# RWKV-7 recurrence of a backbone block: key and value products moved to the idle quarters of the TensorE array

## The reference, cut to what matters

```python
def rwkv7_scan(S0, r, decay, k, v, kk, a, reverse):
    def step(S, inp):
        r_t, w_t, k_t, v_t, kk_t, a_t = inp
        sa = jnp.einsum('bhvk,bhk->bhv', S, -kk_t)
        S = (S * w_t[:, :, None, :] + sa[..., None] * (kk_t * a_t)[:, :, None, :]
             + v_t[..., None] * k_t[:, :, None, :])
        return S, jnp.einsum('bhvk,bhk->bhv', S, r_t)
```

## Time and profile before

| | us |
|---|---|
| median of 3 runs | 2715.4 |
| lowest, highest | 2714.63, 2723.09 |
| the profiled execution | 2723.21 |
| its span | 2721.5 |
| mean granted TensorE clock | 0.928 of full speed |

### The profile page before, as it was taken

How to read it: one execution, slowest core, us unless ns; L and a number is a source line. 1 busy time by engine, 2 the same in 40 slices (tenths; PEclk the granted TensorE clock), 3 DMA queues, 4 the chain that set the end, 5 groups by cost and what they waited for, 6 DMA issues and landing times. The chain is left out here.

```text
span 2721.5 us, 60797 instructions
## 1 busy us (share of the span) xinstructions
PE 2415.9 (89%) x26659; PEld 1980.0 (73%) x26659; DVE 1147.7 (42%) x1601; ACT 804.3 (30%) x1329; POOL 458.1 (17%) x335
## 2 busy tenths in 40 slices
PE   5899985899999999996979999999797777899999
PEld 3668763788888888895868888888574445588887
DVE  4532323555555655643242222222348663433333
ACT  2232322343342343222153211221332332442231
POOL 0221213543543443520000000000111000000000
PEclk8889895799999999997989999999898998999999
DMA  9565650000000000003112221222110002233332
GB/s 309 169 207 176 191 175 24 21 23 9 28 23 8 29 22 9 9 10 124 53 47 62 68 70 56 62 67 64 47 32 23 0 0 62 62 96 105 89 105 84
DMA packets 261694, 191.86 MB, mean 70 GB/s; under 512 B 11610, under 2 KB 251876, under 8 KB 260964
## 3 DMA queue, kind: packets, MB, share of 16 engines
q1 hardware_dynamic: 261476, 188.58, 22.8%
HBM read 170.73 MB, written 17.83 MB: 69 GB/s over the span
## 5 line engine op out<-in xcount | busy, mean ns | idle before, releaser
L493 PE MATMUL bank<-operand_hi,ffn_hi 128*128 128x512 f32 (+1 forms) x1056 | 378.4, 358 | 25.7 <-DVE operand_lo L455 25.7
L486 DVE TENSOR_TENSOR ffn_lo<-ffn_raw,ffn_hi 128x1024 fp32r<-128x1024 f32 (+1 forms) x120 | 159.8, 1332 | 572.0 <-ACT ffn_hi L481 571.9
L494 PE MATMUL bank<-operand_lo,ffn_hi 128*128 128x512 f32 (+1 forms) x1056 | 377.5, 358 | 0.0
L495 PE MATMUL bank<-operand_hi,ffn_lo 128*128 128x512 f32 (+1 forms) x1056 | 374.9, 355 | 0.0
L481 ACT CAST ffn_hi<-ffn_raw 128x1024 fp32r<-128x1024 f32 (+1 forms) x120 | 136.4, 1136 | 531.4 <-PE bank L495 531.2
L1499 POOL TENSOR_TENSOR lvl<-sc,level_mask 128x512 f32<-128x512 f32 x144 | 203.9, 1423 | 441.9 <-PE bank L1124 407.8
L493 PEld LDWEIGHTS bank<-operand_hi,ffn_hi 128*128 128x128 f32 x1056 | 200.3, 190 | 62.7 <-issue 22.4
L495 PEld LDWEIGHTS bank<-operand_hi,ffn_lo 128*128 128x128 f32 x1056 | 199.7, 189 | 29.9
L494 PEld LDWEIGHTS bank<-operand_lo,ffn_hi 128*128 128x128 f32 x1056 | 200.4, 190 | 27.2
L494 PE MATMUL bank<-ffn_g_lo,ffn_hi 128*128 128x512 f32 (+1 forms) x528 | 188.0, 356 | 0.0
L493 PE MATMUL bank<-ffn_g_hi,ffn_hi 128*128 128x512 f32 (+1 forms) x528 | 187.4, 355 | 0.0
(11 more groups left out here) (243 smaller groups left out, 4660.8 us busy)
## 6 DMA issues: line engine op xcount, KB each, us to landing
mod_raw<-in_mod_w SPq DMA_DIRECT2D x96, 512.0 KB, 6.2
ffn_raw<-in_ff_w SPq DMA_DIRECT2D x88, 512.0 KB, 3.9
ffn_raw<-in_ff_w SPq DMA_DIRECT2D x32, 704.0 KB, 4.5
proj_raw<-in_rw_wr SPq DMA_DIRECT2D x8, 512.0 KB, 4.5
proj_raw<-in_rw_wk SPq DMA_DIRECT2D x8, 512.0 KB, 4.6
proj_raw<-in_rw_wv SPq DMA_DIRECT2D x8, 512.0 KB, 5.0
rwkv_out_raw<-in_rw_wo SPq DMA_DIRECT2D x8, 512.0 KB, 3.8
qk_w_raw<-in_at_wq SPq DMA_DIRECT2D x8, 512.0 KB, 3.7
```

The lines of the kernel that those rows point to most:

```text
L486: signal(eng, eng.tensor_tensor(self.lo[s][:, 0:k_tiles, :], self.raw[s][:, 0:k_tiles, :], self.hi[s][:, 0:k_tiles, :].bitcast(F32), ALU.s ...
L493: pe.matmul(out, w[0], x[0], start=first, stop=False)
L494: pe.matmul(out, w[0], x[1], start=False, stop=False)
L495: return pe.matmul(out, w[1], x[0], start=False, stop=last)
```

## The change

The key half of each score, the turned keys and the turned values are written to the other head's partitions, so head 0 uses the upper right quarter of the array and head 1 the lower left one. b and k are issued alternately, into a bank each (`B_BANK`, `K_BANK`), and `sc` splits into `sc_b` and `sc_k`. Scores are made for two steps at a time, two times a group instead of four; VectorE masks each bank on its own, so there are still four masks of 512 columns a group. Keys are turned with b in one call (`turn_keys`).

The three products of a step that need keys and values alone (key scores times values, keys times values, values times key scores for the output) leave `rhs` and `sy`. They are made one step ahead (`early_part`), in the off-diagonal quarters, two matmuls after each of the first six pairs of the inverse's `y`. `CHAIN` becomes two banks that alternate by step, and `rhs` and `sy` add to what `early_part` began. The last slot has no inverse and issues them alone. New waits: `y` waits for the outputs' state products of the present step (`y_opened`), and `rhs` and the output part of `sy` for the early products (`early_done`).

The banks for this come from `SIDE`, `T_BANK` and `X_BANK`: they become two `WORK` banks, through which `t`, `y` and all side pieces rotate, each waiting for the reader of the use before last.

```diff
-        Y_BANK, CHAIN, SIDE, SC_BANK = c.bank[0:2], c.bank[2], c.bank[3], c.bank[4:6]
-        T_BANK, X_BANK = c.bank[6], c.bank[7]
+        Y_BANK, CHAIN, B_BANK, K_BANK, WORK = c.bank[0:2], c.bank[2:4], c.bank[4], c.bank[5], c.bank[6:8]
...
+                def following(q):
+                    return (C, q + 1) if C and q < GROUP - 1 else (B, 0) if B and q == GROUP - 1 else None
...
                 if C:
                     E.u(C, 0)
-                if B:
-                    y(B, 2)
-                if A:
-                    score(A, 1)
+                y(B, 2, following(0))
                 extra(1)
                 if C:
                     E.sy(C, 0)
                 if A:
-                    score(A, 2)
+                    score(A, 1)
                 extra(2)
                 if C:
                     E.rhs(C, 1)
                 if B:
                     t(B, 3), cut(B, 5)
                 if A:
-                    score(A, 3), cut(A, 0), cut(A, 1)
+                    cut(A, 0), cut(A, 1)
                 extra(3)
                 if C:
                     E.u(C, 1)
-                if B:
-                    y(B, 3)
+                y(B, 3, following(1))
                 if A:
-                    turn(A, 0)
+                    turn_keys(A)
...
                 if B:
                     t(B, 4)
                 if A:
-                    level0(A), cut(A, 2), turn(A, 1)
+                    level0(A), cut(A, 2)
                 extra(6)
                 if C:
                     E.u(C, 2)
-                if B:
-                    y(B, 4)
+                y(B, 4, following(2))
                 if A:
-                    turn(A, 2)
+                    turn_values(A)
...
+                    def work_free(self, *key):
+                        n = self.use.of("work", *key)
                         if n >= 2:
-                            kind, g, i = self.use.key["bank", n - 2]
...
+                    def score(self, G, i):
...
+                        for q in (2 * i, 2 * i + 1):
+                            for e in range(2):
+                                n = G.chunk(q, e)
+                                tokens, at = slice(n * CH, n * CH + CH), 128 * (2 * (q % 2) + e)
                                 for h in range(2):
+                                    pe.matmul(B_BANK[half(h), at:at + 2 * CH], b_in[G.pair][e][half(h), tokens],
+                                              ar[G.pair][e][half(h), n, :, :], start=True, stop=True)
+                                for h in range(2):
+                                    mm = pe.matmul(K_BANK[half(1 - h), at:at + 2 * CH], k_in[G.pair][e][half(h), tokens],
                                                    ar[G.pair][e][half(h), n, :, :], start=True, stop=True)
                         mm.then_inc(scores, 1)
...
+                    def y(self, G, n, step):
+                        bank = self.work_free("y", G.g, n)
                         pe.wait_ge(t_copied, self.use.of("t", G.g, n) + 1)
+                        if step:
+                            self.early_waits(*step)
                         for w in range(2 * GROUP):
                             for h in range(2):
-                                mm = pe.matmul(X_BANK[half(h), w * CH:w * CH + CH], t_sb[G.parity][half(h), w, :],
+                                mm = pe.matmul(bank[half(h), w * CH:w * CH + CH], t_sb[G.parity][half(h), w, :],
                                                inv[G.third][half(h), w, :], start=True, stop=True)
+                            if step and w < 6:
+                                self.early_part(*step, w)
                         mm.then_inc(x_ready, 1)
...
+                    def early_part(self, G, q, part):
+
+                        e, m, alone = part % 2, G.step(q), G.j == q == 0
+                        n, w, bank = G.chunk(q, e), 2 * q + e, CHAIN[G.step(q) % 2]
+                        values = vtok[G.pair][:, n, :]
+                        if part < 2:
+                            for h in range(2):
+                                pe.matmul(bank[half(h), e * CH:e * CH + CH], sc_k[G.third][half(1 - h), q, e, 0, :],
+                                          values[half(1 - h), :], start=(e == 0), stop=False, skip_group_check=True)
+                        elif part < 4:
+                            for h in range(2):
+                                mm = pe.matmul(bank[half(h), 256 + e * CH:256 + e * CH + CH], tok[G.third][half(1 - h), 1, w, :],
+                                               values[half(1 - h), :], start=False, stop=False, skip_group_check=True)
+                            if alone and part == 3:
+                                mm.then_inc(rhs_ready, 1)
+                        elif not alone:
+                            self.y_values(G, q, e, early_done)
```

More of the change, by code:

```diff
@@ L862, in schedule, with score, turn_keys, turn_values @@
             use = E.use = Uses()
[L864 to L872, removed]
+            def score(G, i):
+                use.take("bank", "score", G.g, i)
+                E.score(G, i)
+            def turn_keys(G):
+                use.take("bank", "keys", G.g), use.take("turn", "keys", G.g)
+                use.take("copy", "b", G.g), use.take("copy", "k", G.g)
+                E.turn_keys(G)
+            def turn_values(G):
+                if G.j < 2:
+                    use.take("bank", "values", G.g), use.take("turn", "values", G.g), use.take("copy", "v", G.g)
+                    E.turn_values(G)
             def level0(G):
@@ L1012, in nothing @@
                 pass
-            diag = score = turn = level0 = cut = t = y = rhs = u = sy = feature = readout = nothing
+            diag = score = turn_keys = turn_values = level0 = cut = t = y = early = rhs = u = sy = feature = readout = nothing
         def map_piece(n):
@@ L1047, in put @@
                 def put(t):
-                    sp.wait_ge(f_read, use.of("side", t, "gate", 1) + 1)
+                    was_read(sp, use, t, "gate", 1)
                     sp.dma_start(dram[3][:, t, :], gated[:]).then_inc(stored, 16)
@@ new lines, in turn_values @@
+                    def turn_values(self, G):
+                        self.banks_free("values", G.g)
+                        first, count = ((0, GROUP), (GROUP, 2 * GROUP))[G.j]
+                        for n in range(count):
+                            for h in range(2):
+                                mm = pe.matmul(K_BANK[half(1 - h), n * CH:n * CH + CH],
+                                               v_s[G.pair][half(h), (first + n) * CH:(first + n + 1) * CH],
+                                               centre[half(h), :], start=True, stop=True)
@@ new lines, in y_values @@
+                    def y_values(self, G, q, e, done):
+                        n = G.chunk(q, e)
+                        y, out = Y_BANK[n // 8], slice(n % 8 * CH, n % 8 * CH + CH)
+                        opens = (G.j == q == e == 0) or (G.j == 1 and q == 0 and e == 1)
+                        for h in range(2):
+                            mm = pe.matmul(y[half(h), out], vtok[G.pair][half(1 - h), n, :], sc_k[G.third][half(1 - h), q, e, 1, :],
+                                           start=opens, stop=False, skip_group_check=True)
+                        if e == 1:
+                            mm.then_inc(done, 1)
@@ L1480, in diag @@
                         if G.g >= 2:
-                            pool.wait_ge(turned, self.use.of("turn", G.g - 2, 1) + 1)
+                            pool.wait_ge(turned, self.use.of("turn", "keys", G.g - 2) + 1)
                         for e in range(2):
```

330 lines of the change are left out of this document (170 added, 160 removed).

## The result

The kernel after takes 2583.7 us (median of four runs, 2581.9 to 2587.6), the kernel before 2715.0 (four runs, 2710.1 to 2723.1): a ratio of 0.952 with a 95% interval from 0.949 to 0.954, 131 us less. The profiled execution took 2585.16 us with a span of 2583.6, 137.9 less than the span before, at a mean clock of 0.941 (0.928 before).

What follows compares the result with a forecast made beforehand. TensorE was taken to bound the long slots, a GpSimd-to-VectorE chain sharing the middle one. Of 5.47 us a group saved, 2.6 to 3.5 is kept: 98.5 to 87.5 us a pair, 85 us in all, likeliest 2632, range 2590 to 2695.

Steps and rivals of the forecast that it cites:

- the walk: Instruction durations followed through the recurrence's slots: a head pair goes from 98.5 to 87.5 us, 85 us over 7.7 pairs.
- the clock term: Half-clock stretches behind stalls cost 5.3 us of a pair in the recurrence; kept unchanged, 2670 if new waits double it.
- the side pieces' wait for one another: TensorE's side products, each waiting for the reader of the one before; sharing two banks counted at 0.5 to 1 us a pair.
- Do four tiles run at once?: On TensorE, four quarters taken as running at the pace of two; 5.47 us a group less work, 131 us over 24.
- middle slot: Second of a head pair's three slots, with little extra TensorE work; GpSimd's chain binds, 27.1 becomes 25.6 us.
- map slot: Slot of a head pair that carries the next pair's decay maps on TensorE: 36.9 becomes 31.5 us.
- readout slot: Slot of a head pair that carries the readout of the last pair, with the lowest clock: 34.5 becomes 31 us.
- rival D: Stalls smaller than walked and a clock that improves because the readout's waits shrink: 2600; inside the main case's 0.70.
- VectorE's wait for GpSimd's sum: In the middle slot, behind GpSimd's chain of levels and products: to grow from 1.1 to 2 us or more.
- A: Quarters sharing rows or columns do not run together at 64 columns, but the 128-column scores do: 2687, chance 0.10.
- B: Off-diagonal quarters run in turn with the diagonal ones everywhere; 14 us slower, 2730; chance 0.07 with other slower outcomes.
- C: Gain goes into new waits: GpSimd's chain binds all slots, clock falls; half stays, 2675; chance 0.10 up to 2700.

Runs made afterwards that it cites:

- diagonal with side wait: The diagonal kernel, with each side piece of TensorE again waiting until the piece before it is read: 2706.2 us, ratio 0.998.
- diagonal: The kernel after with every product back in its own head's quarter; order, weaving and banks as changed: 2672.1 us, ratio 0.986.
- the turns were moved: The kernel after with the key turn ahead of the third level's y and the value turn ahead of the fourth's: 2582.0 us, ratio 0.952.
- the later sum: VectorE's two operations that wait for GpSimd's sum moved from place 9 to 11 of the middle slot: 2587.6 us in after, 2698.8 us in before.
- turns and `t(B, 5)`: The kernel after with the turns moved ahead of y and `t(B, 5)` ahead of `y(A, 1)`: 2577.7 us, ratio 0.951.
- fillers: The kernel before with eight unread identity products in each of two places of a pair where TensorE idles some 2 us: 2703.1 us, ratio 0.996.
- Blocks: The kernel after with all b products of a score or key-turn call issued ahead of all k products: 2608.6 us, ratio 0.963.
- After with the side wait: The kernel after, four quarters kept, with each side piece of TensorE again waiting until the piece before it is read: 2630.5 us, ratio 0.971.

## Why the prediction was right or wrong

**The sum.** The account from before to after, in us of the profiled executions, each term from a pair of kernels that differ in it:

| term | measured | from | forecast |
|---|---|---|---|
| order, weaving, division of banks, steady, full clock | +14.0 | diagonal with side wait - before | in the walk |
| four quarters, steady, full clock | -89.8 | after - diagonal | in the walk |
| side pieces free of one another, steady, full clock | -11.7 | diagonal - diagonal with side wait | -4 to -8 |
| together | -87.5 | 701.5 to 614.0 | -85 |
| clock, steady | -22 at most | 68.3 to 23.9 us at 1.2 GHz | 0 |
| opening | -24 | 122.5 to 98.9 | 0 |
| outside | -5 | rest of the spans | 0 |

The walk's 85 us stood at full clock, in part by luck: width took 118 us from TensorE and not 131, and 30 of them were lost again and not 46. What was wrong are two steps: the clock term, which the prediction kept as it was ("I keep it"), and the side pieces' wait for one another, counted at 0.5 to 1 us a pair and at nothing in the opening. With the clock's 22 and the opening's 24 us the forecast would have been 2586.

The medians give the same account without any price for the clock: before 2715.0, diagonal with the side wait 2706.2, diagonal 2672.1, after 2583.7. That is 9 us for order, weaving and banks together with the clock that they give back, 34 for the side pieces' freedom, where the forecast had 4 to 8, and 88 for width. With four quarters the side wait costs 47. The first step, 9 us, is hardly clear of noise: its ratio reaches from 0.996 to 1.000.

**Do four tiles run at once?** Right, and it was the step on which everything hung. The forecast had 5.47 us a group from width; the first-to-last starts give 4.91. Of it 2.6 to 3.5 us was to be kept; the 87.5 us over 24 groups are 3.65, or 3.2 without the banks' 11.7.

**Stalls and slots.** The middle slot came out as forecast, 25.2 us for 25.6. The map slot was forecast at 31.5 and is 28.5, the readout slot 31 and 28.7. In the pair shown above the three slots take 81.6 us against 98.5. The clock held 5.3 us of the 98.5 by the prediction's own sum and holds none of the 81.6, which leaves 11.6 at full clock for the 11 forecast. So here too the clock was the missing part: map and readout slot had it, the middle one did not the earlier trace rows. The prediction had seen that the clock falls behind stalls, and that the readout's waits shrink, and gave both only to rival D (2600).

**Which waits.** The forecast wanted TensorE's idle before y at 30 us or more and its wait for the state at 40. The first is 22.4 in the steady part and 26.8 over the whole recurrence, the second 22.3, nearly unchanged from 21.6. The two masks ahead of the state did not lengthen it; only when the turns were moved did it grow (31.7). The reason for the first is as forecast, the bare copy, but the wait is 0.50 us for 0.65, in some 40 places and not in three of every slot. VectorE's wait for GpSimd's sum was forecast to grow from 1.1 to over 2 us a pair; over seven pairs it went from 9.7 / 7 = 1.4 to 11.5 / 7 = 1.6. The reason given for the middle slot, that GpSimd's chain binds it through that sum, fell with the later sum: the wait went and the slot stayed. 25.6 was a right number with a wrong reason, a lucky one, and what binds that slot stays open. TensorE's work has a part in it: without width the slot is 27.7 us (diagonal kernel). No single wait that I moved shortened it by more than 1.2 us (25.2 to 24.0, turns and `t(B, 5)`).

The added waits were taken at nothing, on the ground that they are on TensorE's own results. One that was moved is not: the output's value products now come first and wait for ScalarE to have read the bank, seven times 1.4 us, 10.1 for 2.0 before. The diagonal kernels have the same 10.1, so 8 of the order's 14 us may be this wait; no run took it away.

**Side banks.** Counted at 0.5 to 1 us a pair, measured 11.7 / 8 = 1.5 in the steady part, and 17 to 19 us in the opening; 34 to 47 us in all by the medians. The earlier trace rows already showed the kind of wait, but the prediction read those rows as a matter of the slots and took the first pair's features for covered. In the opening nothing else is there to cover them: its clock was 0.61.

**Rivals.** A (no overlap at 64 columns, 2687) falls by the timeline of after. B's mechanism, order without width, cost 14.0 us at full clock, as worked out, but it would not have given 2730: with the old side wait it gives 2706, since the same order removes long gaps and with them stretches at 1.2 GHz, and with two banks 2672. C (the gain goes into new waits) is true for a quarter of the width: 118 us taken from TensorE, 90 arrive. D, with a better clock, was the nearest; both its conditions came true. TensorE's idle time in the steady part grew by 23 us (59.7 to 82.9), where the sum had 131 - 85 = 46 for new stalls, and the clock rose.

Two things are not settled. Which of the order's moves closed before's long gaps was not taken apart; fillers and the later sum each take away more than half of the time at 1.2 GHz (20.5 and 30.7 us left). And the exact price of a stretch at 1.2 GHz was taken as half its length, which the fillers bear out in the profiled execution (20.2 us gained, 47.8 / 2 = 23.9 by the rule, and the 3.7 between them is what the fillers themselves may cost) and the medians only in part (8 to 11).

## What to carry to other kernels

Where a small product uses a diagonal quarter of the array, a second one in the other quarters cost almost no time here, where the two were issued alternately, and 0.60 to 0.76 of the time taken from TensorE arrived. Before setting a clock term to "unchanged", list the longest gaps and ask for each whether the change closes it: filling two of them per pair gained 20 us of the profiled execution here and 8 to 11 of the median, with more work on TensorE. The list alone does not decide it, since stretches at 1.2 GHz also came without a long gap. And cost the waits of a shared bank in the stretch that has no cover, here the opening, on its own.

## What the runs showed of the hardware that I had not expected

- Records issued behind others started ahead of them in another quarter: six k records beside the last six b records of a block. Blocks therefore lose only a part of the overlap (1.29 us a call, against 0.88 alternating and 1.65 on one diagonal).
- The clock did not follow the idle sum. The diagonal kernel, with 52.6 us idle in its steady part and one gap over 1.5 us, had no stretch at 1.2 GHz there. Before, with 59.7 us and 12 such gaps, had 18 stretches, 68.3 us. After, with 82.9 us and 2 gaps, had 6 stretches, 23.9 us.
- Nor did it follow the long gaps alone. After with the side wait has 2 gaps over 1.5 us, as after does, and 8 stretches, 44.4 us, with 93.2 us idle. The kernel before with fillers has 5 stretches left, of which one stands at a gap over 1.5 us. What else lowers the clock, no run here took apart.
